# A hybrid retention/GLA block on one core: last blocks by row tile, gate sums in fp32r high and low parts

## The reference, cut to what matters

```
log_a = log_sigmoid(a_low @ gla_a_up + bias) / 16        # GLA gates, per token and key column
b     = cumsum(log_a)                                    # the gate sums: prefix sums over tokens
y     = merged @ w_out                                   # output projection, 2048 x 2048
h_state = x + g1 * rms_norm(y, norm_mix_post)
h     = rms_norm(h_state, norm_ffn_pre) * (1 + sc2) + sh2
y     = (silu(h @ ffn_w_gate) * (h @ ffn_w_up)) @ ffn_w_down
out   = h_state + g2 * rms_norm(y, norm_ffn_post)
```

## Time and profile before

| | |
|---|---|
| median of three runs | 1775.55 us |
| the profiled execution, its own time | 1775.38 us |
| its span | 1773.7 us |
| PE busy | 1729.0 us (97%) |
| DVE, ACT, POOL busy | 971.2, 729.3, 162.9 us |
| mean granted clock of TensorE | 0.991 |
| DMA | 415.88 MB, 234 GB/s over the span |

### The profile page before, as it was taken

How to read it: one execution, slowest core, us unless ns; L and a number is a source line. 1 busy time by engine, 2 the same in 40 slices (tenths; PEclk the granted TensorE clock), 3 DMA queues, 4 the chain that set the end, 5 groups by cost and what they waited for, 6 DMA issues and landing times.

```text
span 1773.7 us, 21618 instructions
## 1 busy us (share of the span) xinstructions
PE 1729.0 (97%) x7885; PEld 1392.7 (79%) x7885; DVE 971.2 (55%) x1044; ACT 729.3 (41%) x798; POOL 162.9 (9%) x177
## 2 busy tenths in 40 slices
PE   6999999999999999999999899999999999999997
PEld 3468888887778888888888678888888888888885
DVE  2347666647655676676665544444444444444444
ACT  3222222227446454445454464444444444443442
POOL 0010000000044454230000000000000000000000
PEclk9999999999999999999999999999999999999999
DMA  9999999869888575566767646666666666766662
GB/s 366 387 387 344 340 315 320 315 208 354 286 304 270 170 232 179 172 189 191 237 226 251 188 151 192 189 189 189 189 189 189 188 189 189 260 193 192 195 194 73
DMA packets 181546, 415.88 MB, mean 234 GB/s; under 512 B 12830, under 2 KB 13118, under 8 KB 171632
## 3 DMA queue, kind: packets, MB, share of 16 engines
q1 hardware_dynamic: 156288, 304.14, 53.9%
q10 hardware_dynamic: 17856, 82.43, 12.6%
q0 software_dynamic: 7344, 28.53, 4.7%
HBM read 394.54 MB, written 20.50 MB: 234 GB/s over the span
## 4 chain that ended last, share of the span: by engine, by line
PE 93%; DVE 2%; DMA 2%; issue 1%; ACT 1%; SPq 0%; DVEq 0%; ACTq 0%; POOL 0%; POOLq 0%
PE ps L1362 27%; PE ps L1366 27%; PE ps L1374 27%; PE ps L1435 2%; PE ps L1418 2%; DMA raw<-in_w_mod 1%; PE ps L1620 1%; PE ps L1636 1%; PE ps L1674 1%; DMA xn<-in_x 1%; ACT w_hi L593 1%; PE ps L1715 1%; PE ps L1407 1%; PE ps L1500 0%; PE ps L1591 0%
## 5 line engine op out<-in xcount | busy, mean ns | idle before, releaser
L940 DVE TENSOR_TENSOR w_lo<-raw,w_hi 128x1024 fp32r<-128x1024 f32 x496 | 610.7, 1234 | 544.3 <-ACT w_hi L593 544.2
L593 ACT ACTIVATE w_hi<-raw 128x1024 fp32r<-128x1024 f32 x496 | 525.0, 1060 | 827.3 <-PE ps L1374 797.0
L1362 PE MATMUL ps<-w_hi,h_hi 128*128 128x512 f32 x1504 | 472.9, 396 | 0.0
L1366 PE MATMUL ps<-w_hi,h_lo 128*128 128x512 f32 x1504 | 463.8, 390 | 0.0
L1374 PE MATMUL ps<-w_lo,h_hi 128*128 128x512 f32 x1504 | 410.1, 389 | 0.0
L1366 PEld LDWEIGHTS ps<-w_hi,h_lo 128*128 128x128 f32 x1504 | 282.3, 188 | 59.3
L1374 PEld LDWEIGHTS ps<-w_lo,h_hi 128*128 128x128 f32 x1504 | 282.3, 188 | 59.1
L1362 PEld LDWEIGHTS ps<-w_hi,h_hi 128*128 128x128 f32 x1504 | 278.8, 188 | 57.6 <-issue 2.8
L952 DVE SCALAR_TENSOR_TENSOR acc<-wm,csil,acc 128x2048 f32<-128x2048 f32 (+1 forms) x60 | 141.0, 2350 | 93.8 <-DMA wm<-in_w_mod 93.7
L1362 PE MATMUL ps<-w_hi,hid_hi 128*128 128x512 f32 x352 | 108.4, 389 | 0.0
L1366 PE MATMUL ps<-w_hi,hid_lo 128*128 128x512 f32 x352 | 108.3, 389 | 0.0
(11 more groups left out here) (269 smaller groups left out, 1268.0 us busy)
## 6 DMA issues: line engine op xcount, KB each, us to landing
raw<-in_w_in SPq DMA_DIRECT2D x176, 512.0 KB, 5.5
wm<-in_w_mod ACTq DMA_DIRECT2D x64, 1024.0 KB, 6.9
raw<-in_ffn_w_gate SPq DMA_DIRECT2D x88, 512.0 KB, 4.5
raw<-in_ffn_w_up SPq DMA_DIRECT2D x88, 512.0 KB, 4.4
raw<-in_ffn_w_down SPq DMA_DIRECT2D x88, 512.0 KB, 4.6
raw<-in_w_mod SPq DMA_DIRECT2D x64, 512.0 KB, 7.9
raw<-in_w_out SPq DMA_DIRECT2D x32, 512.0 KB, 4.7
px<-stage ACTq DMA_DIRECT2D x44, 256.0 KB, 6.3
```

The costliest lines, as they stand in the source:

```text
L593: act.activation(w_hi[:, j % SPLIT, :, :], raw[:, j % RAW, :, :], ACT.Copy).then_inc(w_high, 1)
L940: dve.tensor_tensor(w_lo[:, j % SPLIT, :, :], raw[:, j % RAW, :, :], w_hi[:, j % SPLIT, :, :].bitcast(F32), ALU.subtract).then_inc(w_low, 1)
L1362: pe.matmul(o, hi[:, kk, c], w_hi[:, q, e, :], start=kk == 0, stop=False)
L1366: pe.matmul(o, lo[:, kk, c], w_hi[:, q, e, :], start=False, stop=False)
```

## The change

The output projection, the start of the FFN and the end of the down product are cut by row tile; the FFN's start also by a new transposing step. In the last block of `w_out` and of `w_down` the last four slots run all of tile 0, then all of tile 1 (weights are held in the four split buffers; `w_used` is signalled in the second pass, `half_done` after the first). FFN slots 0 to 3 run in the same way; slots 4 to 7 run both tiles. The norms are computed for each tile, `hs` is scaled by DVE into a new buffer `hn`, and PE transposes `hn` in twelve units (`UNITS`). The gate sums run on a high and a low part of `la`, each in fp32r, with a matrix of 258 columns. All pieces of one direction are done ahead of the other's: z at p = 4 and 16, sums at 12 and 24, context sums at 14 and 26. The chunk list ends at slot 34.

```diff
-        base = (cursor[0] + 63) // 64 * 64
+        base = (cursor[0] + 127) // 128 * 128
-        CHUNK_AT = [0, 2, 4, 6, 9, 11, 13, 15, 17, 19, 22, 24, 26, 28, 30, 31]
+        CHUNK_AT = [0, 2, 4, 7, 9, 11, 13, 16, 18, 20, 23, 25, 27, 29, 32, 34]
+        UNITS = [(j, (m,)) for m in range(MT) for j in range(SPLIT)] + [(j, (0, 1)) for j in range(SPLIT, 8)]
+        HN_ORDER = [(0, 0), (0, 1), (1, 0), (1, 1), (0, 2), (1, 2), (0, 3), (1, 3)]
...
 # ACT at_pre
+                if p in (9, 21):
+                    act.wait_ge(S("la_ready"), d + 1)
+                    act.activation(lat_hi[:, :, :], la[:, d, 0:2, :], ACT.Copy).then_inc(S("la_hi_ready"), 1)
+                    act.activation(ctx_hi[:, :, :], la[:, d, 2:4, :], ACT.Copy).then_inc(S("la_hi_ready"), 1)
 # DVE at_pre
+                if p in (10, 22):
+                    for m, hi in ((0, lat_hi), (2, ctx_hi)):
+                        dve.wait_ge(S("la_hi_ready"), 2 * d + m // 2 + 1)
+                        dve.tensor_tensor(la_lo[:, d, m:m + 2, :], la[:, d, m:m + 2, :], hi[:, :, :].bitcast(F32),
+                                          ALU.subtract).then_inc(S("la_lo_ready"), 1)
 # PE at_pre
-                            last = pe.matmul(bank(4 + h)[:, 0:L + 1], la[:, d, m, h * GDK:(h + 1) * GDK],
-                                             before[:, m, :], start=m == 0, stop=m == MT - 1)
+                            pe.matmul(bank(4 + h)[:, 0:L + 2], lat_hi[:, m, c], before[:, m, :], start=m == 0, stop=False)
+                        for m in range(MT):
+                            last = pe.matmul(bank(4 + h)[:, 0:L + 2], la_lo[:, d, m, c], before[:, m, :],
+                                             start=False, stop=m == MT - 1)
...
 # ACT, from the output projection to the FFN
+            square_last(0); split(S_FFN, 0)
+            for n in range(OUT_BLOCKS):
+                square_hs(0, n)
+            split(S_FFN, 1); square_last(1); split(S_FFN, 2)
+            take_h2(0); take_h2(1); split(S_FFN, 3); take_h2(2); square_hs(1, 0); take_h2(3)
+            for n in range(1, OUT_BLOCKS):
+                square_hs(1, n)
+            take_h2(4); take_h2(5)
+            for j in range(4, 8):
+                take_h2(j + 2); split(S_FFN, j)
+            take_h2(10); take_h2(11)
 # DVE
+            mean_squares(0); scale_last(0)
+            for n in range(OUT_BLOCKS):
+                residual(0, n)
+            split(S_FFN, 0); mean_squares_h(0); normal(0); split(S_FFN, 1); mean_squares(1); scale_last(1)
+            low_h2(0); normal(1); split(S_FFN, 2); residual(1, 0); low_h2(1); residual(1, 1); residual(1, 2)
+            low_h2(2); residual(1, 3); split(S_FFN, 3); mean_squares_h(1); low_h2(3); normal(2); normal(3)
+            low_h2(4); low_h2(5); normal(4); normal(5); low_h2(6); normal(6); normal(7)
 # PE
+            for u in range(3):
+                turn_h2(u)
+            for m in range(MT):
+                for j in range(SPLIT):
+                    pe.wait_ge(S("h2_lo_ready"), SPLIT * m + j + 1)
+                    products(S_FFN, j, 2 * j, KT - 1, LAT[m:m + 1], 2 + m, signal=w_used if m == 1 else None)
+                    if m == 0 and j == 0:
+                        turn_h2(3)
+                    if m == 1:
+                        turn_h2(7 + j)
+                if m == 0:
+                    for u in range(4, 7):
+                        turn_h2(u)
+            for j in range(SPLIT, 8):
+                pe.wait_ge(S("h2_lo_ready"), SPLIT + j + 1)
+                products(S_FFN, j, 2 * j, KT - 1, LAT, 2)
+                if j == SPLIT:
+                    turn_h2(11)
```

More of the change, by code:

```diff
@@ new lines, in _ @@
+            split(S_FFN, 0)
+            mean_squares_h(0)
+            normal(0)
+            split(S_FFN, 1)
+            mean_squares(1)
+            scale_last(1)
+            low_h2(0)
+            normal(1)
+            split(S_FFN, 2)
+            residual(1, 0)
+            low_h2(1)
+            residual(1, 1)
+            residual(1, 2)
+            low_h2(2)
+            residual(1, 3)
+            split(S_FFN, 3)
+            mean_squares_h(1)
+            low_h2(3)
+            normal(2)
@@ L1308, in hidden @@
+            normal(3)
+            low_h2(4)
+            low_h2(5)
+            normal(4)
+            normal(5)
+            low_h2(6)
+            normal(6)
+            normal(7)
+            for j in range(4, 8):
+                low_h2(j + 3)
+                split(S_FFN, j)
+            low_h2(11)
             def hidden(j, n):
@@ L1351, in _, with products @@
         def _(pe):
-            def products(s, j, k, last_k, tiles, first_bank, between=None, used=1):
+            def products(s, j, k, last_k, tiles, first_bank, between=None, used=1, signal=w_used):
                 if isinstance(s, int):
@@ L1374, in products @@
                         last = pe.matmul(o, hi[:, kk, c], w_lo[:, q, e, :], start=False, stop=kk == last_k)
-                last.then_inc(w_used, used)
+                if signal is not None:
+                    last.then_inc(signal, used)
             LAT = [(h_hi, h_lo, 0), (h_hi, h_lo, 1)]
@@ L1713, in turn_h2 @@
+            def turn_h2(u):
+                j, ms = UNITS[u]
+                pe.wait_ge(S("hn_ready"), max(HN_ORDER.index((m, j // 2)) for m in ms) + 1)
+                if u >= 4:
+                    pe.wait_ge(S("h2_hi_ready"), u - 3)
                 for e in range(2):
-                    for m in range(MT):
-                        last = pe.matmul(bank(4 + j % 4)[:, e * L + m * P:e * L + (m + 1) * P],
-                                         hs[:, m, (2 * j + e) * P:(2 * j + e + 1) * P], diag[:, m, :], start=True, stop=True)
+                    for m in ms:
+                        last = pe.transpose(bank(4 + u % 4)[:, e * L + m * P:e * L + (m + 1) * P],
+                                            hn[:, m, (2 * j + e) * P:(2 * j + e + 1) * P], ident[:, :])
@@ L1754, in _ @@
                         turn_columns(hid_n, "hid_n_ready", FF_BLOCKS - 1)
+            for m in range(MT):
+                for j in range(DOWN_SLOTS - SPLIT, DOWN_SLOTS):
+                    end = S("half_done") if m == 0 and j == DOWN_SLOTS - 1 else None
+                    products(S_DOWN + (OUT_BLOCKS - 1) * DOWN_SLOTS, j, 2 * j, D_FF // P - 1, HID[m:m + 1], m,
+                             signal=w_used if m == 1 else end)
 STACKED = ["w_mod", "b_mod", "norm_mix_pre", "norm_mix_post", "norm_ffn_pre", "norm_ffn_post", "w_in", "ret_decay",
```

289 lines of the change are left out of this document (175 added, 114 removed).

## The result

The changed kernel takes 1764.68 us (median of four runs: 1764.71, 1764.65, 1764.74 and 1758.22) against 1775.81 us of the kernel before beside it, a ratio of 0.9927 with an interval of 0.9915 to 0.9938. It gains 11.1 us where 14.9 were forecast. The fourth run is 6.5 us under the others; the experiments come back to it.

What follows compares the result with a forecast made beforehand. PE was taken as the bound, busy 1729.0 of 1773.7 us, so only its work or waits count. The terms 8.3 + 3.8 + 6.9 - 1.9 - 2.2 = 14.9 took 1775.4 to 1760.5 us, range 1755.5 to 1767.

Steps and rivals of the forecast that it cites:

- part 4: Chunk list: last chunk moves to slot 34, so PE waits for the DMA of `rows` at p = 46; -2.2 us.
- Part 1: Projection's end (E) to the FFN's first half block: one long wait becomes short ones, ending at E + 35.0; gain 8.3 us.
- no fall of the clock: Upper bound at the projection-to-FFN boundary: clock stays full, half block ends at E + 33.5 (E: projection's end); gain 9.8 us.
- Part 2: The kernel's end: tile 0's share fits under tile 1's pass, leaving 8.1 us behind PE's end; gain 3.8 us.
- Part 3: Gate sums: fp32r matmuls in both directions gain 6.9 us; two waits of 1.0 for `la_lo` cost 1.9.
- Part 5: Alignment: 64-byte rounding already put the base at a multiple of 128, so buffers stay and nothing is gained.
- Rival (a): New waits in gate sums and chunk list don't show: 4.1 us more gain, 1756.4 us; chance 0.15.
- (b): FFN's start: clock stays low until the double slots, E + 40.7; 5.7 us less gain, 1766.2 us; chance 0.11.
- (c): Gate sums: fp32r costs as much as the halves of fp32; 6.5 us less gain, 1767.0 us; chance 0.05.
- (d): FFN's start: clock at 1.2 GHz through the whole half block, ending at E + 55.7; slower, 1781.2 us; chance 0.03.

Runs made afterwards that it cites:

- experiment 3: The kernel before with only the new chunk list (last chunk at slot 34, not 31): 1782.29 us, ratio 1.0036.
- experiment 1: The changed kernel with the old chunk list (last chunk at slot 31): 1758.28 us, ratio 0.9897.
- experiment 6: The changed kernel, new chunk list kept, with POOL's stores of the sum rows and their load moved between the groups of decay operations: 1757.33 us.
- experiment 4: The changed kernel with 20 unused matmuls put ahead of PE's wait for the sum rows at p = 46: 1759.56 us, ratio 0.9913.
- experiment 5: The changed kernel with 40 unused matmuls put ahead of PE's wait for the sum rows: 1762.4 us, ratio 0.9925.
- experiment 7: The changed kernel with the old chunk list and 14 and 17 unused matmuls in PE's two waits between projection and FFN: 1757.24 us.
- experiment 8: experiment 7 plus the low part of unit 3 made ahead of the mean of row tile 1's squares on DVE: 1756.32 us.
- Experiment 10: experiment 6 with only the last slot, not the last four, of the last DOWN block run by row tile: 1759.63 us.
- experiment 2: The kernel before with the gate sums' part of the change alone, old chunk list: 1770.23 us, ratio 0.9966.
- experiment 11: experiment 6 with the base of all regional buffers 64 bytes above a multiple of 128: 1772.85 us, ratio 0.998.
- experiment 12: experiment 6 with only `w_hi` and `w_lo` 64 bytes above a multiple of 128: 1796.85 us, ratio 1.0116.

## Why the prediction was nearly right, and where it was not

**Sign, mechanisms and range** held: 1764.7 lies in 1755.5 to 1767. The level was 4.2 us too low. One term, part 4, was off by 5.2; the other three together came out 0.8 better than forecast and hid some of it.

**Part 4, the chunk list: -2.2 forecast, -6.1 to -7.35 measured** (experiments 3, 1 and 6). The mechanism was right, that PE stands at p = 46 for rows whose load has moved later. Two things were sized wrong. First, the step "`rows` is loaded at 538.41 + 5.4 = 543.8 and lands 3.3 later": it moved the whole chain by the delay and kept its parts. But the stores of `sumd` then ran beside other transfers. POOL's wait for them was 1.88 us before, with the DMA engines 0.69 busy, and 3.94 after, with 1.01 busy; here are both windows, DMA share and GB/s last, first before:

```profile
536.50:538.40 1.90, 1.90 (x10) 1.59 (x9) 0.41 (x2) 1.44 (x3) 0.04 (x1) 1.00 0.69 168
```

```profile
536.30:540.30 4.00, 3.07 (x14) 2.22 (x12) 2.22 (x2) 3.55 (x5) 0.06 (x2) 1.00 1.01 336
```

That, and 0.4 us more for the load, turns the 2.2 us into 4.6. That the share is the cause is the likeliest reading: over POOL's wait it was 0.68 with 1.97 us (experiment 1), 0.79 with 3.17 (experiment 4), 0.96 with 3.56 (experiment 3) and 0.93 with 5.01 (experiment 5). No run varied it alone. Second, the prediction counted a fall of the clock at the boundary and none here, though the wait it forecast was as long: "PE stands 2.2 us in the middle of full work" was priced at 2.2. The low clock costs 2.75 us beyond the wait by experiment 6, some 3.1 to 3.4 by experiment 5, and 1.5 in experiment 3 (6.1 less 4.6). The bound of 4 for this term was too low for the same reasons. The term's other premise, that POOL's twelve durations vary freely, is set right by experiment 4: they follow DVE's splits.

**Part 1, the boundary: 8.3 forecast, 7.8 measured.** The two waits are 1.92 and 2.28 us where 1.9 and 2.4 stood, the clock fell in the second and was back at E + 11, inside the forecast's 9 to 12, and tile 1's first pass waits 1.38 for 1.1. Slot 3 waits 0.46 and not 1.5, since the slots ahead of it ran at half clock. The half block ends at E + 35.5 for 35.0. The half microsecond most likely lies in ACT's small pieces: a square of 512 columns with its read comes every 0.82 us and not 0.70, and `take_h2` on one tile takes 1.15 and not 1.05. The prediction set "no fall of the clock" at E + 33.5; experiment 7 has E + 34.6, and reaches 33.9 only with experiment 8's swap. For `take_h2` the Trainium skill's "VectorE: DVE Perf Modes", section "The TRN2 errata — SBUF-src ops pay a fixed extra latency per instruction", gave an estimate of 0.25 us for 128 columns out of PSUM; the trace has 0.40 (0.80 for two), and the measurement decides. On the Trainium skill's "TensorE: Matmul & The Clock Gate", section "Part 4: PE-mode transpose", the boundary is silent: between the waits and the return of the clock PE ran mostly matmuls. Two small figures of the prediction were misread: ACT's 12.9 us from 16 on end at 28.9 and not 28.6, and in the trace of before the clock was back at 1028.3, behind 4.1 us of work and not 4.9. Neither changes a term.

**Part 2, the end: 3.8 forecast, 4.5 measured.** 7.4 us are left and not 8.1: the sums and the power come within 1.7 us of the square's start, and no gap stands before the four pieces. Experiment 10 confirms the mechanism.

**Part 3, the gate sums: 6.9 less 1.9 forecast, 5.6 measured in the trace** and 6.0 by the median alone (experiment 2). fp32r costs 1.97 and 1.87 a direction where 1.84 and 1.82 stood. The context part's matmuls take 0.233 and not 0.227 each, which is the price of experiments 11 and 12; by the order of the kept buffers in the kernel, `after` starts 32 bytes above a multiple of 128, but no run moved it alone. The wait for `la_lo` came once (0.9) and not twice; with the old list it comes twice (1.1 to 2.1 in experiments 1, 2, 7 and 8), so the new list does help here by 0.2 to 1.2 us, which its other effect buried. The wait that is left is not for the data of the sums: `la_lo` of the latent tokens was done at 428.3 and PE was there at 428.6, but the count that PE waits for (`la_lo_ready` at `2 * d + 2`) includes the context part, which ended at 429.5. Waiting for one less there should remove it; no run tried that.

```profile
427.10 1.22 DVE L1120 TENSOR_TENSOR la_lo<-la,lat_hi 128x1024 fp32r<-128x1024 f32 x1
428.24 1.22 DVE L1120 TENSOR_TENSOR la_lo<-la,ctx_hi 128x1024 fp32r<-128x1024 f32 x1
```

**Part 5, alignment: nothing, as forecast**, for the reason given: nothing moved. What such an offset would cost was not asked, and it is large (experiments 11 and 12).

**Ledger.** 7.8 + 4.5 + 5.6 - 4.6 - 2.75 = 10.55. These terms are read from the two profiled executions, whose spans differ by 10.7 (1773.7 to 1763.0), so the ledger closes to 0.15. The 11.1 of the medians is larger because the runs of the kernel before beside it had a median of 1775.81, 0.4 above its profiled execution. Rival (a), that the new waits don't show, is probably the run of 1758.22, one of four; (b) to (d) did not happen.

## What to carry to other kernels

When a step is moved later, its transfers are to be timed anew beside what runs then; and a new wait of PE in full work is to be priced with the half clock that may stand behind it, which added 1.5 to 3.4 us to the wait of 4.6 us here. POOL operations beside DVE's splits are to be timed against these splits, and not by a mean: a start 0.6 us later made the chain of twelve 2.0 us longer. Without slack behind it such a chain seems to make the time two-valued (1764.7 or 1758.2 us); issuing the stores in the middle of the chain (experiment 6) cost nothing and gave 7.35 us. A wait that cannot be removed can be filled with unused matmuls, which gives something only where no other chain sets the next start.

## What the runs showed of the hardware

- An fp32r matmul of 512 columns takes 0.227 us with both operands at a multiple of 128 bytes and 0.233 with the weights or the moving operand 64 bytes off: 15.5 us where it touches a quarter of this kernel's matmuls (experiment 11), 39.5 us where it touches 6528 of 7853 (experiment 12). Both together were not tried, nor which offsets other than 64 do it.
- A POOL operation on 128x512 that starts while DVE splits weights (two inputs, 128x1024) ends 1.15 us (the sum) or 1.43 us (a product) after the split; alone it takes 1.29 or 1.56. So the same operation takes 1.3 to 2.6 us, and twelve of them took 19.8 or 21.8 us (experiment 4 and after).
- Half clock followed a single wait of 4.6 us; behind it stood some 6 us of uninterrupted work at half clock in after and 3.4 in experiment 3. With only 1.0 us of waiting at the same place it never came (experiment 5), and single waits of 1.57 and 1.66 us early in after (to 52.23 and to 111.87) left the clock at 1.00.
- The same three stores of 12 KB held POOL for 1.9 us (before) to 5.0 us (experiment 5).
